# Attention without dividing its probabilities, and convolution projections set between retention heads, in a three-block kernel on one Trainium2 core

## The reference, cut to what matters

```python
# first block, 8 heads; 256 local and 256 context keys per query in one softmax
p = jax.nn.softmax(jnp.concatenate([s_loc, s_ctx], axis=-1), axis=-1).astype(v.dtype)
o = (jnp.einsum('bhrqk,brkhd->brqhd', p[..., :n_loc], vb)
     + jnp.einsum('bhrqk,bkhd->brqhd', p[..., n_loc:], v_ctx))

# second block, each of 2 layers
y_mla = mla_branch(...)        # 8 heads, softmax over 512 keys, values of 64 channels
y_conv = conv_branch(...)      # gate a * sigmoid(g), 31 taps over positions, norm, silu, projection
y_ret = retention_branch(...)  # 4 heads, keys of 128, values of 256, decay by distance
merged = gates[:, :, 0] * y_mla + gates[:, :, 1] * y_conv + gates[:, :, 2] * y_ret
```

## Time and profile before

| what | value |
|---|---|
| median of 3 runs | 3071.1 us (3070.17 to 3073.45) |
| the profiled execution | 3070.77 us, span 3069.0 us |
| PE busy | 2867.2 us, 93% of the span |
| DVE busy | 1416.2 us, 46% |
| ACT busy | 1202.2 us, 39% |
| POOL busy | 1218.1 us, 40% |
| granted clock of PE, mean | 0.967 |
| attention of the first block | about 271 to 493 us |
| MLA attention, layer 0 and layer 1 | 1021 to 1221 us and 2074 to 2272 us |

### The profile page before, as it was taken

One profiled execution on the slowest core, in us unless ns is written; L12 is line 12 of the kernel. 1 busy time (PEld: TensorE's weight loads), 2 busy tenths in 40 slices (PEclk: granted clock), 3 DMA queues, 4 the chain that ended last, 5 costly groups with the idle time before them and its releaser, 6 DMA issues.

```text
span 3069.0 us, 33644 instructions
## 1 busy us (share of the span) xinstructions
PE 2867.2 (93%) x13132; PEld 2242.5 (73%) x13132; DVE 1416.2 (46%) x1887; ACT 1202.2 (39%) x1737; POOL 1218.1 (40%) x555
## 2 busy tenths in 40 slices
PE   8997899899999988999998999979799999899997
PEld 4776677688887756677786888857476777778886
DVE  5656554431113788644515202278977363251123
ACT  4346653342223454333334222254544333342222
POOL 1122233344444454343444444434534433354442
PEclk9998999899999999999999999989899999999998
DMA  6333222232223111122231222221011222222221
GB/s 232 107 126 115 73 90 89 101 115 96 96 97 130 69 42 42 54 91 76 83 124 70 102 96 96 97 101 67 25 56 69 89 80 92 96 89 97 96 96 62
DMA packets 89374, 278.08 MB, mean 91 GB/s; under 512 B 10048, under 2 KB 10240, under 8 KB 89216
## 3 DMA queue, kind: packets, MB, share of 16 engines
q1 hardware_dynamic: 89216, 275.92, 25.0%
HBM read 268.54 MB, written 7.34 MB: 90 GB/s over the span
## 4 chain that ended last, share of the span: by engine, by line
PE 76%; DVE 16%; ACT 5%; issue 2%; DMA 1%; POOL 0%; SPq 0%; DVEq 0%; ACTq 0%; POOLq 0%
PE bank L1416 23%; PE bank L1418 22%; PE bank L1417 22%; PE bank L1641 2%; DVE pageF L2334 2%; PE bank L1467 1%; PE bank L1602 1%; DVE pageF L2408 1%; DVE pageF L2412 1%; ACT L1685 1%; DVE pageR L2207 1%; DVE smal L2116 1%; PE bank L1614 1%; PE bank L1632 1%; PE bank L1454 1%
## 5 line engine op out<-in xcount | busy, mean ns | idle before, releaser
L2444 POOL TENSOR_TENSOR wlo<-wraw,whi 128x1024 fp32r<-128x1024 f32 x429 | 1048.1, 2445 | 1602.0 <-ACT whi L1668 1594.4
L1416 PE MATMUL bank<-pageR,whi 128*128 128x512 f32 x3552 | 1446.1, 407 | 73.0 <-ACT pageR L1828 27.4
L1417 PE MATMUL bank<-pageR,whi 128*128 128x512 f32 x3552 | 1385.6, 390 | 0.0
L1418 PE MATMUL bank<-pageR,wlo 128*128 128x512 f32 x3552 | 1385.4, 390 | 0.0
L1416 PEld LDWEIGHTS bank<-pageR,whi 128*128 128x128 f32 x3552 | 677.3, 191 | 255.2 <-issue 105.7
L1417 PEld LDWEIGHTS bank<-pageR,whi 128*128 128x128 f32 x3552 | 678.0, 191 | 152.2 <-issue 23.8
L1418 PEld LDWEIGHTS bank<-pageR,wlo 128*128 128x128 f32 x3552 | 676.3, 190 | 140.8
L1668 ACT ACTIVATE whi<-wraw 128x1024 fp32r<-128x1024 f32 x429 | 450.7, 1053 | 410.9 <-PE bank L1418 406.3
L1708 ACT ACTIVATE pageR<-pageF 128x512 fp32r<-128x512 f32 x136 | 85.9, 632 | 432.9 <-DVE pageF L2201 208.2
L2334 DVE SCALAR_TENSOR_TENSOR pageF<-pageF,prm 128x497 f32<-128x497 f32 (+9 forms) x180 | 202.7, 1126 | 1.8
L1467 PE MATMUL bank<-cst,pageF 128*128 128x128 f32 x564 | 88.3, 284 | 60.1 <-ACT pageF L1790 40.4
(11 more groups left out here) (197 smaller groups left out, 2202.1 us busy)
## 6 DMA issues: line engine op xcount, KB each, us to landing
wraw<-in_wst SPq DMA_DIRECT2D x429, 512.0 KB, 3.4
pageF<-in_wmod SPq DMA_DIRECT2D x96, 256.0 KB, 4.7
pageF<-in_xT SPq DMA_DIRECT2D x16, 256.0 KB, 4.9
pageF<-in_bias SPq DMA_DIRECT2D x16, 256.0 KB, 4.2
kept<-pageF SPq DMA_DIRECT2D x16, 256.0 KB, 4.8
pageF<-kept SPq DMA_DIRECT2D x16, 256.0 KB, 4.1
pageF<-tables SPq DMA_DIRECT2D x8, 256.0 KB, 4.3
out_x<-pageF SPq DMA_DIRECT2D x8, 256.0 KB, 2.0
```

Of the source, the lines that this page charges most:

```text
L1416: e.matmul(o, hi, xh, start=first, stop=False)
L1417: e.matmul(o, hi, xl, start=False, stop=False)
L1418: i = e.matmul(o, lo, xh, start=False, stop=last)
L2444: e.tensor_tensor(wlo[:, b % NH, :, :], wraw[:, b % NR, :, :], bc(whi[:, b % NH, :, :]), ALU.subtract).then_inc(*wlod.up(("wlo", b)))
```

## The change

First, the probabilities are no longer divided by their row sums before they meet the values. `soft_norm` is gone; the exponentials go to the transposes as they are. The sums of eight jobs stand side by side, and one reciprocal of 128 x 8 is taken for all eight (`soft_sums`). When a pair of heads is done, `soft_rows` spreads its eight columns over a PSUM bank: for each, one product of the column, broadcast to 64 columns, with the identity, so that each query's reciprocal stands on all the 64 partitions of its head. DVE multiplies the pair's page by that bank (`na_out`, `mla_out`), and `halves` now waits for this multiplication.

Second, in each layer of the second block the main line takes the convolution's projections 0 and 3, then retention head 0, the convolution's 1, head 1, the convolution's 2, where it took 0, 1, 2, 3 and then both heads.

`weave` takes a rate instead of a divisor (0.25 for 4), which leaves the order as it was.

```diff
@@ attention
-            if 1 <= i <= n:
-                step("soft_norm", kind, jobs[i - 1], (i - 1) % 8)
             yield
             if i < n:
                 j = jobs[i]
                 middle(j)
                 pages.take(("pr", kind, j))
-                step("soft_exp", kind, j, i % 8)
+                step("soft_exp", kind, j, i)
                 sbk.give(("sc", kind, j), ("pr", kind, j))
+            if i % 8 == 0 and i:
+                step("soft_sums", kind, jobs[i - 1], i // 8 - 1)
             if 2 <= i < n + 2:
                 j = jobs[i - 2]
-                to_tokens(("pt", kind, j), ("pr", kind, j), ALL4, sbk, ("prn", kind, j))
+                to_tokens(("pt", kind, j), ("pr", kind, j), ALL4, sbk, ("pr", kind, j))
...
+    def soft_rows(kind, pair, n):
+
+        sbk.take(("rs", kind, pair))
+        step("soft_rows", kind, pair, n)
@@ the end of a pair of MLA heads (the first block's is alike)
-                    pages.take(("o_mla_f", l, j))
-                    step("evict", ("o_mla_f", l, j), ("mlab", l, j), 512)
-                    sbk.give(("mlab", l, j), ("o_mla_f", l, j))
-                    p.halves(("o_mla", l, j), ("o_mla_f", l, j), ("o_mla_f", l, j), "pool")
+                    soft_rows("mla", (l, j), j)
+                    evict(("o_mla_f", l, j), ("mlab", l, j), 512, sbk)
+                    step("mla_out", l, j)
+                    sbk.give(("rs", "mla", (l, j)), ("o_mla_n", l, j))
+                    p.halves(("o_mla", l, j), ("o_mla_f", l, j), ("o_mla_n", l, j), "pool")
@@ the main line of a layer
-        weave(chain(main_mla(), main_conv(), main_ret(0), main_ret(1), main_branch(0, "o_mla", 4, "w_mo"),
-                    main_branch(1, "o_conv", 4, "w_pw"), main_ret(2), main_ret(3),
+        weave(chain(main_mla(), main_conv(0), main_conv(3), main_ret(0), main_conv(1), main_ret(1), main_conv(2),
+                    main_branch(0, "o_mla", 4, "w_mo"), main_branch(1, "o_conv", 4, "w_pw"), main_ret(2), main_ret(3),
                     main_branch(2, "o_ret", 8, "w_ro")),
@@ PE
+            def soft_rows(kind, pair, n):
+                o = bank(("rs", kind, pair))
+                clear(("rs", kind, pair))
+                w.wait_ge(*when("rc", kind, *pair))
+                for qt in range(4):
+                    for hp in range(2):
+                        c = 224 + 8 * (n % 2) + 2 * qt + hp
+                        i = e.matmul(o[64 * hp:64 * hp + 64, 128 * qt:128 * qt + 128],
+                                     smal[:, c:c + 1].broadcast_to([128, 64]), ident, start=True, stop=True)
+                i.then_inc(*dot.up(("rs", kind, pair)))
@@ DVE
-            def soft_norm(kind, job, i):
-                _, sm, rc = stat(i)
-                P = F(("pr", kind, job))
+            def soft_sums(kind, job, n):
+                o = 8 * (n % 2)
                 w.wait_ge(*when("pr", kind, job))
-                e.reciprocal(rc, sm).then_inc(*vec.up())
-                after()
-                e.tensor_scalar(P, P, rc, None, ALU.mult).then_inc(*vec.up(("prn", kind, job)))
+                e.reciprocal(smal[:, 224 + o:232 + o], smal[:, 208 + o:216 + o]).then_inc(*vec.up(("rc", kind, *job[:-2], job[-2] // 2)))
...
+            def mla_out(l, j):
+                o = F(("o_mla_f", l, j))
+                w.wait_ge(*when("o_mla_f", l, j))
+                w.wait_ge(*when("rs", "mla", (l, j)))
+                e.tensor_tensor(o, o, bank(("rs", "mla", (l, j))), ALU.mult).then_inc(*vec.up(("o_mla_n", l, j)))
```

More of the change, by code:

```diff
@@ L135, in give, with weave @@
         self.free.append(self.place[name])
-def weave(main, sides, every):
+def weave(main, sides, rate):
     sides = [s for s in sides]
-    n = 0
+    due = 0
     for _ in main:
-        n += 1
-        if n % every == 0:
+        due += rate
+        while due >= 1:
+            due -= 1
             sides = [s for s in sides if next(s, "end") != "end"]
@@ L877, in side_tables @@
         yield
-    weave(main_ffn("", H2, out_x, norm_x2()), [side_tables()], 4)
+    weave(main_ffn("", H2, out_x, norm_x2()), [side_tables()], 0.25)
     def layer(l, rs, feed):
@@ L1008, in side_mla, with main_conv @@
                 yield
[L1010 to L1021, removed]
+        def main_conv(m):
+            bks = sbk if m == 0 else mb
+            yield from proj("w_cg" + L, m, X, bks=bks)
+            tanh_scaled(("ca", l, m), ("o", "w_cg" + L, m), bks)
+            yield from proj("w_ca" + L, m, X, bks=bks)
+            pages.take(("cap", l, m))
+            step("scaled", ("cap", l, m), ("o", "w_ca" + L, m), rs.r)
+            bks.give(("o", "w_ca" + L, m), ("cap", l, m))
+            step("glu", ("ca", l, m), ("cap", l, m))
+            pages.give(("cap", l, m), ("glu", ("ca", l, m)))
+            made.add(("ca", l, m))
         def taps(m):
@@ L1304, in blocks, with top, total @@
             return ap.rearrange("p (j f) -> p j f", j=4)
-        def stat(i):
-            o = 80 + 4 * i
-            return [smal[:, o + x:o + x + 1] for x in range(3)]
+        def top(i):
+            return smal[:, 80 + i % 8:81 + i % 8]
+        def total(i):
+            return smal[:, 208 + i % 16:209 + i % 16]
         def state(g, c):
@@ L1645, in tensor @@
                 mm, mod_mm, warm_up, mod_columns, square_sum, to_tokens, mod_sum, gla_gate, gla_gate_ctx, gla_state0, gla_states, gla_scores,
-                gla_out, na_scores, na_values, mla_scores, mla_values, conv_mean, ret_scores, ret_values)}
+                gla_out, na_scores, na_values, mla_scores, mla_values, soft_rows, conv_mean, ret_scores,
+                ret_values)}
             for kind, *what in p.steps:
@@ L1786, in soft_exp @@
             def soft_exp(kind, job, i):
-                nm, sm, _ = stat(i)
                 clear(("pr", kind, job))
                 w.wait_ge(*when("mx", kind, job))
-                e.activation(F(("pr", kind, job)), bank(("sc", kind, job)), ACT.Exp, bias=nm, accum_out=sm).then_inc(
-                    *fun.up(("pr", kind, job)))
+                e.activation(F(("pr", kind, job)), bank(("sc", kind, job)), ACT.Exp, bias=top(i),
+                             accum_out=total(i)).then_inc(*fun.up(("pr", kind, job)))
             def na_out(m):
@@ L2111, in soft_exp @@
             def soft_exp(kind, job, i):
-                nm, _, _ = stat(i)
                 w.wait_ge(*when("sc", kind, job))
@@ L2115, in soft_exp, with na_out @@
                     w.wait_ge(*when("sb", *job))
-                e.tensor_reduce(nm, bank(("sc", kind, job)), AX, ALU.max, negate=True).then_inc(
+                e.tensor_reduce(top(i), bank(("sc", kind, job)), AX, ALU.max, negate=True).then_inc(
                     *vec.up(("mx", kind, job)))
-            def soft_norm(kind, job, i):
-                _, sm, rc = stat(i)
-                P = F(("pr", kind, job))
+            def soft_sums(kind, job, n):
+                o = 8 * (n % 2)
                 w.wait_ge(*when("pr", kind, job))
-                e.reciprocal(rc, sm).then_inc(*vec.up())
-                after()
-                e.tensor_scalar(P, P, rc, None, ALU.mult).then_inc(*vec.up(("prn", kind, job)))
+                e.reciprocal(smal[:, 224 + o:232 + o], smal[:, 208 + o:216 + o]).then_inc(*vec.up(("rc", kind, *job[:-2], job[-2] // 2)))
+            def na_out(m):
+                o, r = F(("o_na_f", m)), bank(("rs", "na", (m,)))
+                w.wait_ge(*when("o_na_f", m))
+                w.wait_ge(*when("rs", "na", (m,)))
+                e.tensor_tensor(by64(o), by64(o), by8(r), ALU.mult).then_inc(*vec.up(("o_na_n", m)))
+            def mla_out(l, j):
[3 more added lines that the diff above has]
+                e.tensor_tensor(o, o, bank(("rs", "mla", (l, j))), ALU.mult).then_inc(*vec.up(("o_mla_n", l, j)))
             def silu_gate(h):
```

6 lines of the change are left out of this document (4 added, 2 removed).

## The result

The changed kernel takes 3029.64 us (median of 4 runs, 3027.54 to 3032.71), beside 3071.65 us for the kernel before on the same chip: a ratio of 0.9864 (95% interval 0.985 to 0.9878), 42 us less. Forecast were 24 us less, 3047 us, with a range down to 3030. The execution profiled spans 3025.9 us, before 3069.0.

The account below looks back on a forecast made before the run. The prediction took the MLA parts' thin stretches to be DVE's queue, the rest PE-bound. Layers -15.8 and -13.7, first block +3.4 and +2 behind the MLA parts gave -24.1 us: 3047 us, range 3030 to 3064.

Parts of the forecast that it names:

- What bounds the kernel: Second block's MLA parts: the 60.1 us stretch of lone jobs is a DVE queue with PE hanging on it; elsewhere PE-bound.
- The undivided probabilities: Both blocks' attention: about 12.7 us leaves DVE's queue in a thin stretch; `soft_rows` adds 4.4 us per attention of four pairs.
- +3.4: First block's attention: four groups of `soft_rows` add 4.4 us, 1 us taken off for a wait; bounds -3 and +8.
- The sum: Whole kernel: -15.8 and -13.7 for the two MLA parts, +3.4 first block, +2 behind them: -24.1 us, 3047 us.
- PE idle 8 us: New thin stretch of each layer: 33.7 us long with 25.8 us of PE work, so PE idles 8 us.
- PE's work: Layer 0's MLA part: 89.0 + 47.4 + 31.9 + 4.4 = 172.7 us; layer 1 from 88.6, 46.3, 40.91 x 0.83, 4.4.
- +2: Behind the two MLA parts: heads' side work starts with DVE further behind and PE barely covered, +1 us each.
- So this part by itself moves the thin stretch rather than removes it: New projection order in the second block: lone jobs remain, but at the end, 10 of them; no work comes or goes.
- A: Thin stretch nearly closes: idle falls from 8 to 2 us, the start's 3.2 closes; 3029 to 3037 us; chance 0.20.
- B: DVE sets the dense part, its taps dearer beside conv 3's taps: 5 us a layer, 3057 us; chance 0.17.
- C: Short idle pieces keep PE at half clock through the new thin stretch: 3083 us, or 3057 for half; chance 0.10.
- D: Each pair's end becomes a round trip over PE, DVE and ACT, up to 5.3 us for 12 pairs; chance 0.10.

Follow-up runs that it names:

- the first two expectations: Undivided probabilities with the old projection order, then the new order with divided probabilities, each half of the change against the kernel before: 3057.47 us and 3040.97 us.
- four kernels: Against the changed kernel: weave rate 1.15, 1.4 and 1.05, then gates allowed from 5 free pages: 3053.56, 3061.94, 3033.05 and 3035.32 us.

## Why the prediction came out short

*What bounds the kernel: right.* The lone stretch before was DVE's queue with PE on it. Over the kernels its length was DVE's busy time there plus 2.3 to 6.0 us: 60.1 for 54.6, 50.2 for 44.8, 48.6 for 42.6, 40.3 for 35.5, 38.4 for 35.6, 38.3 for 36.0, 35.1 for 32.5, 33.3 for 27.3, 31.4 for 27.3, 31.1 for 26.9, 29.5 for 24.1. At the lower end PE's own work counts as well, as the doubled `soft_rows` showed (33.3 for 31.1).

*The undivided probabilities: right.* The price of DVE's multiplication was its load. The row of `soft_rows` shows 1.07 us, forecast 1.09; but the row begins 0.2 us before that of the products ahead of it ends, so 0.88 was the right entry for a sum. The first block's attention was forecast at +3.4 us. It was 1.7 us longer in this execution, and 0.8 to 4.2 us longer (2.7 on average) in the nine kernels that have this first block, with single executions of each: the term holds, within a spread as large as itself.

*The sum: this step failed, in the size of three terms, of which idle PE is the first.* The forecast's span was 19.0 us too long.

The first term is "PE idle 8 us" in the new thin stretch. It was 4.25 us, and 4.23 in the second layer, 7.5 us together. A ratio of span to DVE taken from the old stretch and 2 us for the drain were both charged. With 1 us more of PE busy there than forecast, the stretch was 31.1 us for 33.7.

The second term is PE's work, put at 172.7 us in layer 0 and at 173.3 in layer 1; PE was busy for 170.1 and 170.9, 5.0 us less together. 1.7 of this are the eight groups of `soft_rows` at 0.88 in place of 1.09. Another 1.2 is the end of the old thin stretch, the first 2.5 us of the piece taken at its face value of 47.4, which ran at the half clock and is gone. Most of the rest is in the stretches that were multiplied by their clock of 0.82 and 0.83, a share of the whole time and not of PE's busy time: PE's instructions ran at half clock for 14.9 of 38.9 us and for 16.9 of 40.9, which makes 31.5 and 32.5 us of work, not 31.9 and 34.0. What did not change is the half clock in the dense start of each layer, before and after:

```profile
1021.50:1036.50 15.00, 11.80 (x42) 8.62 (x41) 13.56 (x16) 5.97 (x10) 6.83 (x3) 0.89 0.19 70
1173.80:1176.30 2.50, 2.50 (x8) 1.99 (x7) 2.43 (x6) 1.76 (x5) 0.00 (x0) 0.51 0.00 0
2074.60:2094.60 20.00, 16.80 (x61) 12.65 (x60) 17.50 (x21) 7.93 (x14) 7.08 (x3) 0.83 0.23 79
```

```profile
1024.50:1039.50 15.00, 11.79 (x43) 8.64 (x42) 13.33 (x15) 6.54 (x11) 7.95 (x4) 0.89 0.19 71
2053.70:2073.70 20.00, 16.80 (x60) 12.67 (x59) 17.36 (x20) 8.35 (x15) 8.16 (x4) 0.83 0.23 80
```

These two terms are the 12.5 us by which the two MLA parts came below the sum (177.6 for 183.9, 178.3 for 184.5).

The third term is the "+2" behind the MLA parts, where 1.9 and 2.3 us were gained, 6.2 us away from the forecast. The waits of 4.9, 2.1 and 2.9 us stand there as before. Behind the first part most of the gain is PE's busy time on the same products, 112.3 us for 113.5 up to the same product, where the clock came back some products sooner after a wait. No run shows that this belongs to the change. The parts before the first MLA part came to +3.0 us, forecast +3.4, but by a step that is not the change's.

*"So this part by itself moves the thin stretch rather than removes it": wrong as a ranking of the two halves.* The sum did not use it, but the first two expectations did, and it failed there: the order alone is 30 of the 42 us. The prediction had the mechanism in hand (22 jobs beside projections, taps at 0.742 us without POOL), and gave 28.8 us of DVE and 25.8 of PE for the new stretch; 26.9 and 26.85 came. What it lacked was the price of a lone job. The old stretch took 60.1 us for its 13 lone jobs, 4.6 each, where PE's own work in them was 2.14 each by the prediction. By the maxima in it they were 14, at 4.3 and 2.0; the count changes nothing in the argument.

*The rivals.* A's number came, at its lower edge, but by luck: idle did not go down to 2 us nor did the start's 3.2 close, and what made up for them was the shorter PE work and the 4.2 us behind the MLA parts, which it did not count. B's mechanism happened without its price: the taps beside the PE-bound work rose to 1.255 us, and PE's waits there stayed at 3.2. The Trainium skill (SBUF — State Buffer, section "Who interferes with whom") has the two engines share one port pair as an exclusive lock; the taps at 0.769 us with POOL idle, 0.966 with 12 additions of it and 1.088 with 17 agree. C did not come: clock 1.00. D did not come: ACT stood for the multiplication of the output for at most 1.1 us at each of the twelve pairs, 11.7 us in all.

## What to carry to other kernels

In a stretch where one engine hangs on another's queue, find what fills that queue, and whether a third engine stretches each entry; moving work on the third away may give more than deleting entries. Order is worth more than it looks where covered jobs cost their own work and lone ones their round trip: price a job both ways before calling a reordering a mere move. When "work" is summed from busy rows, the half clock has to be taken off the instructions that ran at it, not off the whole stretch by its mean; and it has to be asked of each such piece whether the change removes it, as at the end of the old thin stretch, or leaves it, as at the start of each layer. Filling the last gap gained nothing in four kernels: each lost more elsewhere, or as much.

## What the hardware showed unexpectedly

- Twelve POOL additions of 1.45 us on unrelated tiles made 24 DVE taps 4.7 us longer (0.966 against 0.769 us each).
- DVE's `tensor_scalar` of 128x512 fp32 took 0.486 to 0.531 us with POOL nearly idle and 0.824 beside POOL's taps: it suffers as the taps do. Two others of this shape, in the lone stretch, took 0.484 us, and 0.809 once the twelve POOL additions were there.
- fp32 products whose weights are one column broadcast to 64 cost what others do: 0.88 us for 8, with 0.14 us for a weight load.
